# Input projection work placed between the units of linear attention, with gate values and six query tiles kept in DRAM meanwhile

## The chip, the cores and the metric

The kernel runs on one core of a Trainium2 chip. The metric is device microseconds (us) of one execution. The core has five engines that run their own instruction streams in order and meet at semaphores: TensorE (PE, with its weight loads as PEld), VectorE (DVE), ScalarE (ACT), GpSimd (POOL) and SyncE (SP, here only a queue that issues DMAs).

## The reference, cut to what matters

One inference step of a one-layer backbone: a modulated norm, one input projection, two head groups that read it, an output projection and a mixture of experts. Tokens are 128 of context and 1024 latent ones. The part around the change:

```
h = modulate(rms_norm(xc, norm_attn_g[l]), sh1, sc1)
q_g, k_g, v_g, g_g, lora, q_s, k_s, v_s = split_cols(h @ w_in[l])
gla_out, s_f, s_b = gla_branch(q_g, k_g, v_g, g_g, lora, s_zero, s_zero, *gla_p)
...
def gla_branch(...):
    la_f = log_gate(lora_f, wa_f, ba_f)
    la_b = log_gate(lora_b, wa_b, ba_b)
    o_f, s_f = gla_chunked(q, k, v, la_f, s0_f)
    o_b, s_b = gla_chunked(flip(q), flip(k), flip(v), flip(la_b), s0_b)
    o = rms_norm(o_f + flip(o_b), norm_g)
    gate = jax.nn.silu(g.reshape(b, t, GLA_HEADS, GLA_DV).astype(jnp.float32))
    out = (o * gate).reshape(b, t, GLA_WIDTH).astype(g.dtype)
```

The columns of `w_in` have the widths 256, 256, 512, 512, 32, 512, 128, 128 for q, k, v and gate of the gated linear attention (GLA), its low-rank gate input, and q, k, v of the windowed attention. GLA needs q, k, v and the low-rank input; its gate is used only at its very end. The windowed attention's q, k, v are not used in GLA at all. Everything is float32.

## The kernel before

All 1152 tokens are nine tiles (NT) of 128. The program is a row of stages; each closes with a barrier of all engines, so nothing of a stage starts before the last work of the stage ahead. Three stages touch the change.

`project` makes four pieces of modulation (`ada`), normalises and transposes the tokens into `hT`, and runs the projection in the order of its list `items`: q and k (`qk`, three groups of three tiles by four column blocks), `lora`, then `vg`, `gg` and `qs` (nine tiles each, 512 columns) and `kv` (nine tiles, 256 columns). For each tile TensorE runs eight matmuls over the model dimension into one of three banks `psP`, and ScalarE or VectorE moves the bank to its place in SBUF (`by_act`: all `gg`, with Silu, and every second of the others by ScalarE). Weights go through a ring of three buffers `wring` that the SP queue fills.

`linear_attention` works in twelve units `UNITS`: three groups `g` of three tiles by four `m` (direction and pair of heads). For unit `u`:

- TensorE `pre(u)`: gate matmul into the single bank `ps_pre`
- ScalarE `soft(u)`: four activations to `lg`, `ng`; VectorE `cumulate(u)`: running sums and differences into `cum`, `fac`; ScalarE `factors(u)`: exponentials in `fac`
- GpSimd: products `pr`, `kz` and `qi`; VectorE `decayed_keys(u)`: `ksT`
- TensorE `scores(u)` into `ps_a`, `turn_keys(u)` into `ps_kt`; VectorE `keep_scores(u)` copies to `AT`; ScalarE `move_keys(u)` copies `ps_kt` to `ks`
- TensorE `delta(u)` into `ps_d`, kept by VectorE as `S`; after the fourth unit of a group TensorE's `intra(g)` forms `AT` times values

`lg`, `ng`, `pr`, `ksT`, `ks` and `ps_a` have two buffers, so products of a unit can run beside the scores of the one ahead. After the units VectorE runs the recurrence over the tiles (`recur`) and TensorE adds the share of the states tile by tile in `ORDER`. GpSimd closes with `gg` times the norm weights (L654). The order of the work is that in which each engine's code is written.

`window_attention` (L790) turns queries and keys, and per tile does scores, softmax, outputs. Between tiles `ada` (L990) makes eight more pieces of modulation from a ring of three 2 MB buffers `ada_ring`; the same SP queue writes 20 MB of zeros to `sum_rows`. The queue order there is:

```
sp.dma_start(ring[i % RING][:], dram["w_ada"]...[:, :, c0:c0 + 512]).then_inc(ring_in[i % RING], 16)
...
for k in range(*((2 * i, 2 * i + 2) if i < 2 else (i + 2, i + 3))):
```

Of the kernel before, what the change touches and what calls it, by code (L numbers as in the profile page):

```python
# [5 lines left out]
F32 = mybir.dt.float32  # L6
BF16 = mybir.dt.bfloat16
I32 = mybir.dt.int32
ALU = mybir.AluOpType
# [22 lines left out]

def cond_of(t):

    return 0 if t == 0 else 1


def project(nc, dram, keep):

    with ExitStack() as ctx:  # L40
# [6 lines left out]
        RING = 3  # L47
# [3 lines left out]
        row = [sb(f"ada_row{i}", [P, 512]) for i in range(2)]  # L51
        ring = [sb(f"wring{i}", [P, KD, 512]) for i in range(RING)]
        NX = 3
        xin = sb("xin", [P, NX, D])
        xn = sb("xn", [P, 2, D])
        junk = sb("junk", [P, D])
# [3 lines left out]
        hT = sb("hT", [P, KD, T])  # L60
# [8 lines left out]
        ring_in = [sem(f"ring_in{i}") for i in range(RING)]  # L69
# [6 lines left out]
        out_done = sem("kv_out_done")  # L76
# [6 lines left out]
        items = [("ada", i) for i in range(4)]  # L83
        items += [("qk", C_QK), ("lora", C_LORA), ("vg", C_VG), ("gg", C_GG), ("qs", C_QS), ("kv", C_KV)]

        def landed(eng, n):
            eng.wait_ge(ring_in[n % RING], 16 * (n // RING + 1))


        outs = []  # L90
        for kind, what in items:
            if kind in ("qk", "lora"):
                for g in range(3):
                    for m in range(4 if kind == "qk" else 1):
                        outs.append((kind, m, g))
            elif kind != "ada":
                for t in range(NT):
                    outs.append((kind, 0, t))

        def used(eng, n):  # L100

            if items[n][0] == "ada":
                eng.wait_ge(ada_done, items[n][1] + 1)
            else:
                eng.wait_ge(proj_done, max(k for k, o in enumerate(outs) if o[0] == items[n][0]) + 1)

        def dest(kind, m, t):
            if kind == "qk":
                return keep["qkT"][:, m, t * 384:(t + 1) * 384]
            if kind == "lora":  # L110
                return keep["loraT"][:, t * 384:(t + 1) * 384]
            if kind == "qs":

                return keep["qs"][:, t, :].rearrange("p (r g d) -> p g r d", r=4, g=2)
            return keep[kind][:, t, :]

        def source(kind, k):
            if kind == "lora":
                return psP[:, k % NB, 0:384]
            if kind == "qs":  # L120
                return psP[:, k % NB, :].rearrange("p (g r d) -> p g r d", r=4, g=2)
            return psP[:, k % NB, 0:{"qk": 384, "kv": 256}.get(kind, 512)]
# [10 lines left out]
        def _(sp):  # L133
            for n, (kind, what) in enumerate(items):
                if n == 0:
                    sp.dma_start(vec[:], dram["vectors"]).then_inc(vec_in, 16)
                    sp.dma_start(keep["ident"][:], dram["ident"]).then_inc(ident_in, 16)
                if n >= RING:
                    used(sp, n - RING)
                c0, cn = (what * 512, 512) if kind == "ada" else what  # L140
                src = w_ada if kind == "ada" else w_in
                sp.dma_start(ring[n % RING][:, :, 0:cn], src[:, :, c0:c0 + cn]).then_inc(ring_in[n % RING], 16)
# [4 lines left out]
                if n == 4:  # L147
# [5 lines left out]
                    sp.wait_ge(wab_zero, 1)  # L153
                    for strip in range(4):
                        sp.dma_start(keep["wab"][32 * strip:32 * strip + 16, 0:256], dram["gla_wa_f"]).then_inc(later_in, 16)
                        sp.dma_start(keep["wab"][32 * strip + 16:32 * strip + 32, 256:512], dram["gla_wa_b"]).then_inc(later_in, 16)
                    sp.dma_start(keep["gla_mask"][:], dram["gla_mask"]).then_inc(later_in, 16)
                    sp.dma_start(keep["normg"][:], dram["gla_norm_g"].to_broadcast([P, P])).then_inc(later_in, 16)
                    sp.dma_start(keep["S0"][:, 0:2, :], dram["state_f"].rearrange("(m p) v -> p m v", p=P)).then_inc(later_in, 16)
                    sp.dma_start(keep["S0"][:, 2:4, :], dram["state_b"].rearrange("(m p) v -> p m v", p=P)).then_inc(later_in, 16)  # L160

            kv0 = outs.index(("kv", 0, 0))
            sp.wait_ge(evac_act if by_act(kv0) else evac_dve, evacs_before(kv0 + 1, by_act(kv0)))
            sp.dma_start(dram["new_k"], keep["kv"][:, 0, 0:128]).then_inc(out_done, 16)
            sp.dma_start(dram["new_v"], keep["kv"][:, 0, 128:256]).then_inc(out_done, 16)
            sp.wait_ge(out_done, 32)
            sp.wait_ge(later_in, 192)

        @block.tensor
        def _(pe):  # L170
# [4 lines left out]
            def ada(n, i):  # L175

                landed(pe, n)
                if i >= 2:
                    pe.wait_ge(row_kept, i - 1)
                for j in range(KD):  # L180
                    strip = slice(32 * (j % 4), 32 * (j % 4) + 32)
                    last = pe.matmul(psT[strip, i % 2, 0:512], condT[:, j, :], ring[n % RING][:, j, :],
# [23 lines left out]
            for n, (kind, what) in enumerate(items):  # L206
# [9 lines left out]
                landed(pe, n)  # L216
                w = ring[n % RING]
                for kk in range(k, len(outs)):
                    if outs[kk][0] != kind:
                        break  # L220
# [11 lines left out]
                    for j in range(KD):  # L232
                        bank = psP[:, kk % NB, 0:512] if kind == "qs" else source(kind, kk)
# [6 lines left out]
                        else:  # L240
                            last = pe.matmul(bank, hT[:, j, t * P:(t + 1) * P],  # L241
                                             w[:, j, 0:what[1]], start=(j == 0), stop=(j == KD - 1))
# [104 lines left out]
def linear_attention(nc, dram, keep):  # L347
# [9 lines left out]
    with ExitStack() as ctx:  # L357
# [12 lines left out]
        UNITS = [(g, m) for g in range(NG) for m in range(4)]  # L370
# [4 lines left out]
        wab, mask, normg, S0 = keep["wab"], keep["gla_mask"], keep["normg"], keep["S0"]  # L375
        restart = sb("restart", [P, W])
        lg = [sb(f"lg{i}", [P, W]) for i in range(2)]
        ng = [sb(f"ng{i}", [P, W]) for i in range(2)]
# [8 lines left out]
        pr = [sb(f"pr{i}", [P, 4, W]) for i in range(2)]  # L387

        kz = [sb(f"kz{i}", [P, 3, W]) for i in range(4)]
        ksT = [sb(f"ksT{i}", [P, W]) for i in range(2)]  # L390
        ks = [sb(f"ks{i}", [P, G, P]) for i in range(2)]
# [3 lines left out]
        AT = [sb(f"AT{m}", [P, G, 2, P]) for m in range(4)]  # L395
        S = sb("S", [P, 4, NT, P])
        ps_pre = ps("ps_pre", [P, 512])

        ps_a = [ps(f"ps_a{i}", [P, 2, 512]) for i in range(2)]
        ps_t = ps("ps_kt", [P, 512])  # L400
        ps_d = ps("ps_d", [P, 512])
        ps_o = ps("ps_o", [P, 512])

        ps_i = [ps_a[i][:, :, 0:2 * DV].rearrange("p h (m v) -> p h m v", v=DV) for i in range(2)]
# [5 lines left out]
        zeroed, next_in = sem("gla_zeroed"), sem("att_const_in")  # L410
# [23 lines left out]
        def _(sp):  # L434
            sp.dma_start(keep["sink"][:], dram["sink"].to_broadcast([P, 8])).then_inc(next_in, 16)
# [12 lines left out]
        def _(pe):  # L448
# [8 lines left out]
            def scores(u):  # L457
# [4 lines left out]
                if u >= 2:  # L462
                    pe.wait_ge(at_done, u - 1)
# [1852 lines left out]
```

## Time and profile before

| | us |
|---|---|
| median of 3 runs | 1713.17 (1712.33 to 1713.4) |
| the profiled execution | 1710.73 |
| its span | 1708.9 |
| TensorE busy in the span | 1533.5 (90%) |
| VectorE, ScalarE, GpSimd busy | 750.8, 522.4, 591.6 |
| projection, from the start | 334.7 |
| linear attention | 168.9 |
| window attention | 162.2 |

The span runs from the first to the last instruction on the engines. The stages' borders are the starts of the first instruction behind each barrier. In a row of the timeline the first number is the start in us, the second the time to the end of the last of the instructions merged in it, and the bracket the idle time of the engine just before, with what ended it. A float32 matmul shows as two records. A row of a stretch gives busy us and the number of records for each engine, then TensorE's granted clock as a share of 2.4 GHz, the busy share of the DMA engines and GB/s.

### The profile page before, as it was taken

What the parts mean: (1) busy time and instruction counts of PE and PEld (TensorE: products, weight loads), DVE (VectorE), ACT (ScalarE), POOL (GpSimd) and SP (SyncE); (2) the same over time, 40 slices, a digit from 0 to 9 for tenths busy, and PEclk for the clock granted to TensorE, in tenths of its full rate; (3) what the DMA queues carried; (4) which work ended last, traced back from release to release, by engine and by line L of the source; (5) the groups of instructions that cost most, each with busy time, mean ns of one, the idle gap of its engine ahead of it and who ended that gap; (6) DMA issues with size and microseconds to landing.
All of it is one profiled execution on the core that took longest, in us unless ns stands there. A gap on an engine that the chain in (4) does not pass through costs nothing. (4 is left out here: it accounts for less than half of the span.)

```text
span 1708.9 us, 28670 instructions
## 1 busy us (share of the span) xinstructions
PE 1533.5 (90%) x9111; PEld 910.9 (53%) x9112; DVE 750.8 (44%) x1478; ACT 522.4 (31%) x1226; POOL 591.6 (35%) x617
## 2 busy tenths in 40 slices
PE   5999999868769999999999869999999999999734
PEld 2554444646656878455555435555555555555311
DVE  2300000187645656278783324444344444444339
ACT  2400000176506663111110023343343334333312
POOL 0000000076655321111124435555455555555422
PEclk8999999957778999999999979999999999999878
DMA  8320000000019903201200079999999999996477
GB/s 322 104 99 0 25 0 0 30 1 8 1 63 411 380 35 154 92 25 50 86 1 0 0 283 333 338 335 331 343 342 329 336 328 307 263 246 125 70 277 301
DMA packets 93495, 289.50 MB, mean 169 GB/s; under 512 B 12190, under 2 KB 15602, under 8 KB 93170
## 3 DMA queue, kind: packets, MB, share of 16 engines
q1 hardware_dynamic: 66210, 199.96, 30.6%
q0 software_dynamic: 25920, 83.91, 20.4%
q10 hardware_dynamic: 1296, 4.72, 0.7%
q8 instruction: 42, 0.69, 0.2%
q14 instruction: 27, 0.22, 0.0%
HBM read 222.09 MB, written 76.94 MB: 175 GB/s over the span
## 5 line engine op out<-in xcount | busy, mean ns | idle before, releaser
L1952 PE MATMUL ps_g<-w_exp,mix 128*64 x1408 | 326.5, 385 | 5.9 <-DVE own_gu L2047 2.8
L1955 PE MATMUL ps_g<-own_gu,mix 128*64 128x256 f32 x1408 | 326.5, 385 | 0.0
L1952 PEld LDWEIGHTS ps_g<-w_exp,mix 128*64 128x64 f32 x1408 | 187.3, 138 | 107.8 <-issue 11.0
L241 PE MATMUL psP<-wring,hT 128*128 128x512 f32 (+1 forms) x576 | 216.7, 539 | 0.0
L1901 POOL DMA_INDIRECT sum_rows<-mix,scatter_row x66 | 143.5, 2175 | 171.9 <-DVE mix L1990 145.4
L1955 PEld LDWEIGHTS ps_g<-own_gu,mix 128*64 128x64 f32 x1408 | 187.3, 138 | 0.0
L1924 PE MATMUL ps_y<-w_exp,hidT 128*64 x352 | 171.4, 610 | 6.4 <-ACT own_d L2003 6.4
L1925 PE MATMUL ps_y<-own_d,hidT 128*64 128x512 f32 x352 | 171.4, 610 | 0.0
L241 PEld LDWEIGHTS psP<-wring,hT 128*128 128x128 f32 x576 | 109.4, 190 | 107.6 <-issue 103.9
L2047 DVE COPY own_gu<-w_exp 128x2048 f32 x89 | 109.5, 1230 | 62.2 <-issue 39.7
L1874 POOL DMA_INDIRECT mix<-h_rows,gather_row x92 | 98.5, 1071 | 79.0 <-POOL gather_row L1871 40.3
L1326 PE MATMUL ps_o<-wo,mixT 128*128 128x512 f32 x288 | 125.2, 592 | 0.5 <-DVE h L1579 0.5
L628 POOL MEMSET kz<- 128x1152 f32 x4 | 4.0, 1054 | 334.8 <-POOLq L2194 334.8
L1916 PE MATMUL ps_x<-ident,mix 128*128 128x128 f32 x712 | 103.8, 289 | 13.8 <-DMA mix<-h_rows,gather_row 13.8
L1916 PEld LDWEIGHTS ps_x<-ident,mix 128*128 128x128 f32 x712 | 86.7, 194 | 48.5 <-issue 33.8
L2003 ACT ACTIVATE own_d<-w_exp 128x1024 f32 x88 | 93.2, 1059 | 51.5 <-issue 48.6
L2059 DVE SCALAR_TENSOR_TENSOR hid<-silu,tab,ps_g 128x128 f32<-128x128 f32 x88 | 30.6, 347 | 159.7 <-ACT silu L2024 159.7
L1326 PEld LDWEIGHTS ps_o<-wo,mixT 128*128 128x128 f32 x288 | 54.0, 190 | 65.3 <-issue 65.3
L1990 DVE COPY mix<-ps_y 128x512 f32<-128x512 f32 x66 | 45.6, 691 | 80.2 <-PE ps_y L1925 80.2
L1982 DVE COPY mix<-ps_x 128x512 f32<-128x512 f32 x89 | 61.6, 692 | 39.0 <-PE ps_x L1916 39.0
L2003 ACT ACTIVATE mix<-ps_x 128x512 f32<-128x512 f32 x89 | 53.1, 597 | 80.3 <-PE ps_x L1916 80.3
L1924 PEld LDWEIGHTS ps_y<-w_exp,hidT 128*64 128x64 f32 x352 | 41.2, 137 | 68.1 <-issue 57.6
(320 smaller groups left out, 2533.1 us busy)
## 6 DMA issues: line engine op xcount, KB each, us to landing
w_exp<-in_exp_w_gate SPq DMA_DIRECT2D x64, 512.0 KB, 7.6
w_exp<-in_exp_w_up SPq DMA_DIRECT2D x64, 512.0 KB, 12.7
w_exp<-in_exp_w_down SPq DMA_DIRECT2D x64, 512.0 KB, 21.5
sum_rows<-zero_row SPq DMA_DIRECT2D x10, 2048.0 KB, 20.7
sums<-sum_rows SPq DMA_DIRECT2D x36, 512.0 KB, 16.3
ada_ring<-in_w_ada SPq DMA_DIRECT2D x8, 2048.0 KB, 18.7
wring<-in_w_ada SPq DMA_DIRECT2D x4, 2048.0 KB, 14.6
wring<-in_w_in SPq DMA_DIRECT2D x4, 2048.0 KB, 10.7
```

Source lines behind the costliest of these rows:

```text
L241: last = pe.matmul(bank, hT[:, j, t * P:(t + 1) * P], w[:, j, 0:what[1]], start=(j == 0), stop=(j == KD - 1))
L1326: last = pe.matmul(ps_o[:, n, :], mixT[t % 2][:, j, :], wo[:, j, n * 512:(n + 1) * 512], start=(j == 0), stop=(j == KD - 1))
L1874: pool.indirect_dma_start(out=x[k], out_offset=None, in_=dram["h2"], in_offset=bass.IndirectOffsetOnAxis(ap=gi[k][:], axis=0), bounds_chec ...
L1901: pool.indirect_dma_start(out=dram["y"][k % 2], out_offset=bass.IndirectOffsetOnAxis(ap=si[k][:], axis=0), in_=y[k], in_offset=None, bound ...
L1916: last = pe.transpose(ps_x[:, j * P:(j + 1) * P], x[k][:, j:D:KD], keep["ident"][:])
L1924: pe.matmul(ps_y[0:HALF, cols], hT[par][:, 0:HALF], w[:, slot * 3 + 2, cols], start=True, stop=True)
L1925: last = pe.matmul(ps_y[HALF:P, cols], hT[par][:, HALF:P], own_d[:, cols], start=True, stop=True)
L1952: pe.matmul(ps_g[par][0:HALF, 0:2 * FF].rearrange("p (k f) -> p k f", k=2), xT[par][:, j * P:j * P + HALF], w[:, bass.ds(slot * 3, 2), ff] ...
L1955: last = pe.matmul(ps_g[par][HALF:P, 0:2 * FF].rearrange("p (k f) -> p k f", k=2), xT[par][:, j * P + HALF:(j + 1) * P], own_gu[par][:, :, ...
L1982: copy(xT[par][:, half * 512:(half + 1) * 512], ps_x[:, half * 512:(half + 1) * 512]).then_inc(done, 1)
L2003: return act.activation(out, in_, ACT.Copy)
L2047: dve.tensor_copy(own_gu[par][:], w[:, bass.ds((e % NW) * 3, 2), :]).then_inc(own_gu_done, 1)
```

## The change

- `project` keeps `qk`, `lora`, then `gg`, and of `vg` only the three tiles of group 0, as six half tiles of 256 columns (VG_EARLY). Its scratch moves into SBUF that later holds other things; the fourth modulation piece has a buffer of its own (`late`), `lora` too.
- GpSimd multiplies each `gg` tile with the norm weights in `project`, and SP stores the tile to the DRAM tensor `gg_rows`. `window_attention` loads the nine tiles again. Their SBUF holds the states `S` in between.
- The rest are 39 portions (`FILL`) of 256 columns that TensorE runs in `linear_attention`: `vg` half tiles of groups 1 and 2 (12), `qs` half tiles (18), `kv` (9). Six stand between the first gate matmuls, two or three in each of the units 0 to 10 (PER_UNIT, 30), three behind the last values. ScalarE copies each out of one of two half banks `ps_f`. SP loads the weights of the portions during the stage into two halves of `late`.
- `qs` tiles 3 to 8 have no place in SBUF then: ScalarE copies them to three staging buffers, SP stores them to `qs_rows`, `window_attention` loads them.
- To make room, `lg`, `ng`, `pr`, `ksT`, `ks`, `ps_a` become single and `kz` goes from four to two; units run in the order m = 0, 2, 1, 3; `pre` runs three units ahead, not four; `factors(u + 2)` stands ahead of `move_keys(u)`, and `delta(u)` in unit u's own turn.
- In `window_attention` the queue also loads `band` and `cache_v`, which came in the stage before.

```diff
-        items += [("qk", C_QK), ("lora", C_LORA), ("vg", C_VG), ("gg", C_GG), ("qs", C_QS), ("kv", C_KV)]
...
+        ITEMS = [("ada", 0), ("ada", 1), ("ada", 2), ("ada", 3), ("qk", 0), ("lora", 0), ("gg", 0), ("vg", 0), ("vg", 1)]
...
+            for t in range(NT):
+
+                sp.wait_ge(gg_scaled, t + 1)
+                sp.dma_start(dram["gg_rows"][t * P:(t + 1) * P, :], keep["gg"][:, t, :]).then_inc(gg_out, 16)
+            sp.wait_ge(later_in, 16 * 14)
+            sp.wait_ge(gg_out, 16 * NT)
...
+        FILL = [("vg", half, t) for g in (1, 2) for half in range(2) for t in range(g * G, g * G + G)]
+        FILL += [("qs", half, t) for half in range(2) for t in range(NT)] + [("kv", 0, t) for t in range(NT)]
...
+        PER_UNIT = (3, 3, 2, 3, 3, 3, 2, 3, 3, 3, 2)
+        START_FILL = 6
...
+                    if k >= 2:
+                        pe.wait_ge(fill_kept, k - 1)
+                    for j in range(KD):
+                        last = pe.matmul(fill_bank(k), hT[:, j, t * P:(t + 1) * P], keep["late_half"](half)[:, j, :],
+                                         start=(j == 0), stop=(j == KD - 1))
+                    last.then_inc(fill_done, 1)
...
-                if u >= 2:
-                    pool.wait_ge(score_done, u - 1)
+                if u >= 1:
+                    pool.wait_ge(score_done, u)
...
+                at = START_FILL + sum(PER_UNIT[:u])
+                keep_fill(at)
+                if u + 2 < NU:
+                    factors(u + 2)
+                move_keys(u)
+                if u < NU - 1:
+                    keep_fill(at + 1)
                 if u + 3 < NU:
                     soft(u + 3)
-                if u + 2 < NU:
-                    factors(u + 2)
+                if u < NU - 1:
+                    keep_fill(at + PER_UNIT[u] - 1)
+            keep_fill(NF)
```

**TensorE at the start of linear attention.** Before; `ps_pre` is the gate bank, `ps_a` the scores, `ps_kt` the turned keys:

```order
L454 MATMUL ps_pre<-loraT,wab 128x384 x4
L471 MATMUL ps_a<-pr,kz 128x4x16 x2
...
L486 MATMUL ps_a<-pr 64x64 x6
L495 MATMUL ps_kt<-ident,ksT 128x128 x3
L454 MATMUL ps_pre<-loraT,wab 128x384
```

Now; `ps_f` is the portions' bank (16 matmuls are two portions), `ps_td` holds turned keys and the state update:

```order
L512 MATMUL ps_pre<-loraT,wab 128x384
L502 MATMUL ps_f<-late,hT 128x256 x16
...
L528 MATMUL ps_a<-pr,kz 128x4x16 x2
...
L543 MATMUL ps_a<-pr 64x64 x6
L512 MATMUL ps_pre<-loraT,wab 128x384
L551 MATMUL ps_td<-ident,ksT 128x128 x3
L502 MATMUL ps_f<-late,hT 128x256 x8
L565 MATMUL ps_td<-vg,ks 64x128 x6
L502 MATMUL ps_f<-late,hT 128x256 x16
```

One portion now stands between the key turn and the state update that needs the moved keys, and two behind it, ahead of the next scores.

**ScalarE, one unit in the middle of the stage.** Before; `ks` is the key move, `lg` and `ng` the gate activations, `fac` and `elast` the factors:

```order
L604 ACTIVATE elast<-gla_off 128x3
L610 ACTIVATE ks<-ps_kt 128x384
L575 ACTIVATE lg<-ps_pre,vcol 128x384
...
L578 ACTIVATE lg<-lg 128x384
L588 ACTIVATE fac<-fac 128x384
```

Now:

```order
L677 ACTIVATE elast<-gla_off 128x3
L683 ACTIVATE ks<-ps_td 128x384
L705 ACTIVATE vg<-ps_f 128x256
L648 ACTIVATE lg<-ps_pre,vcol 128x384
...
L651 ACTIVATE lg<-lg 128x384
L705 ACTIVATE vg<-ps_f 128x256 x2
L661 ACTIVATE fac<-fac 128x384
```

Three copies of portions stand in a unit's row of activations, one ahead of the gate activations and two ahead of the next factors.

**SP at the start of window attention.** Before:

```order
L875 DMA ada_ring<-in_w_ada 128x8x512
L880 DMA sum_rows<-zero_row 128x4x1024 x2
```

Now:

```order
L977 DMA band<-in_band 128x896
L978 DMA cache_v<-in_cache_v 128x128
L975 DMA mix<-qs_rows 128x512 x2
L984 DMA mix<-gg_rows 128x512 x3
L975 DMA mix<-qs_rows 128x512 x2
L990 DMA ada_ring<-in_w_ada 128x8x512
L995 DMA sum_rows<-zero_row 128x4x1024 x2
L984 DMA mix<-gg_rows 128x512 x3
L975 DMA mix<-qs_rows 128x512 x2
L990 DMA ada_ring<-in_w_ada 128x8x512
```

Loads of 256 KB a tile stand ahead of each of the first pieces of the ring.

## Rows read from the trace of the kernel before

**Rows 1.** Stretches: projection, linear attention, window attention; busy us, records, clock, DMA.

```profile
0.00:334.70 334.70, 311.07 (x985) 164.03 (x986) 36.40 (x87) 45.14 (x99) 0.20 (x4) 0.98 0.20 71
334.70:503.60 168.90, 121.87 (x1340) 99.36 (x1341) 117.57 (x226) 88.28 (x266) 105.04 (x134) 0.70 0.03 9
503.60:665.80 162.20, 153.27 (x1254) 119.09 (x1254) 92.17 (x298) 96.81 (x307) 62.94 (x75) 0.95 0.61 234
```

**Rows 2.** Groups of instructions by form; then the stretch of the last key/value tiles.

```profile
L241 PE MATMUL psP<-wring,hT 128*128 128x256 f32 x144 | 31.2, 379 | 0.0
...
L654 POOL TENSOR_TENSOR mix<-mix,normg 128x512 f32<-128x512 f32 x9 | 11.1, 1277 | 0.0
...
306.40:334.60 28.20, 27.54 (x128) 23.91 (x126) 1.70 (x4) 1.87 (x5) 0.00 (x0) 1.00 0.02 5
```

**Rows 3.** Timeline of TensorE, one unit at full clock; then that stretch.

```profile
410.72 0.44 PE L471 MATMUL ps_a<-pr,kz 64*128 64x64 f32 x4
...
413.69 0.55 PE L495 MATMUL ps_kt<-ident,ksT 128*128 128x128 f32 x3
...
415.63 0.44 PE L471 MATMUL ps_a<-pr,kz 64*128 64x64 f32 x4
...
410.60:418.70 8.10, 8.07 (x163) 6.81 (x161) 7.73 (x19) 1.76 (x6) 2.05 (x3) 1.00 0.01 2
```

**Rows 4.** Waits of TensorE in linear attention; first and last scores in the timeline.

```profile
PE ps_a L471 <- POOL kz L647: 13.2, 7, 3.5
...
356.66 0.69 PE L471 MATMUL ps_a<-pr,kz 64*128 64x64 f32 x4 [3.51 <-POOL kz L647]
...
471.65 0.69 PE L471 MATMUL ps_a<-pr,kz 64*128 64x64 f32 x4 [3.02 <-POOL kz L647]
```

**Rows 5.** Timelines of ScalarE, GpSimd and VectorE in linear attention.

```profile
333.98 0.38 ACT L284 ACTIVATE kv<-psP 128x256 f32<-128x256 f32 x1 [6.52 <-PE psP L241]
...
363.98 0.53 ACT L588 ACTIVATE fac<-fac 128x384 f32<-128x384 f32 x1 [4.72 <-DVE fac L708]
...
368.79 0.47 ACT L610 ACTIVATE ks<-ps_kt 128x384 f32<-128x384 f32 x1
369.16 0.57 ACT L575 ACTIVATE lg<-ps_pre,vcol 128x384 f32<-128x384 f32 x1
...
357.52 3.83 POOL L641 TENSOR_TENSOR pr<-qkT,fac 128x192 f32<-128x192 f32 x4
...
365.23 1.00 POOL L650 TENSOR_TENSOR qi<-qkT,fac 128x384 f32<-128x384 f32 x1
...
341.74 0.56 DVE L682 SCALAR_TENSOR_TENSOR ng<-ng,lg 128x384 f32<-128x384 f32 x1 [2.29 <-ACT lg L578]
...
345.07 0.36 DVE L708 TENSOR_SCALAR fac<-fac 128x384 f32<-128x384 f32 x1
...
356.71 1.67 DVE L694 TENSOR_TENSOR_SCAN lg<-restart,ng 128x384 f32<-128x384 f32 x1 [3.71 <-POOL kz L647]
...
363.24 0.71 DVE L708 TENSOR_SCALAR fac<-fac 128x384 f32<-128x384 f32 x1
```

**Rows 6.** Stretches: three value products, the first state output, and what follows.

```profile
480.80:488.20 7.40, 5.89 (x48) 5.51 (x48) 7.36 (x19) 0.00 (x0) 2.95 (x3) 1.00 0.00 0
488.20:493.20 5.00, 2.06 (x32) 1.86 (x32) 5.00 (x16) 0.00 (x0) 0.00 (x0) 0.92 0.00 0
493.20:499.10 5.90, 5.83 (x54) 5.87 (x56) 2.21 (x4) 0.00 (x0) 0.00 (x0) 0.50 0.01 3
```

**Rows 7.** Timeline of TensorE, the ring's first uses; the stretch up to the second.

```profile
518.35 3.64 PE L990 MATMUL ps_k<-ada_ring,condZ 128*32 128x512 f32 x16
...
532.71 1.92 PE L990 MATMUL ps_k<-ada_ring,condZ 128*32 128x512 f32 x16
...
549.48 1.92 PE L990 MATMUL ps_k<-ada_ring,condZ 128*32 128x512 f32 x16
...
503.60:532.70 29.10, 21.90 (x137) 14.70 (x137) 12.67 (x55) 16.50 (x61) 22.66 (x31) 0.71 0.99 377
```

More of the change, by code:

```diff
@@ L50, in project @@
         modA1 = sb("modA1", [P, KD, 2])
[L51 to L52 removed]
+        row = [keep["gg"][:, NT - 2 + i, :] for i in range(2)]
+        slots = [sb(f"wring{i}", [P, KD, 512]) for i in range(3)]
+        slots.append(keep["late"][:].rearrange("p (j n) -> p j n", n=512))
+        wlora = sb("wlora", [P, KD, 32])
+        normg = sb("normg", [P, P])
         NX = 3
[L54 removed]
+        xin = keep["mix"][:, NT * 512:NT * 512 + NX * D].rearrange("p (i n) -> p i n", n=D)
+        junk = keep["mix"][:, NT * 512 + NX * D:NT * 512 + (NX + 1) * D]
         xn = sb("xn", [P, 2, D])
[L56 removed]
         ssq = sb("ssq", [P, NT])
@@ L81, in project @@
         w_in = dram["w_in"].rearrange("(j p) n -> p j n", p=P)
-        items = [("ada", i) for i in range(4)]
-        items += [("qk", C_QK), ("lora", C_LORA), ("vg", C_VG), ("gg", C_GG), ("qs", C_QS), ("kv", C_KV)]
[L86 to L105, printed above, removed]
+        ITEMS = [("ada", 0), ("ada", 1), ("ada", 2), ("ada", 3), ("qk", 0), ("lora", 0), ("gg", 0), ("vg", 0), ("vg", 1)]
+        item_in = [sem(f"w_in_{kind}{i}") for kind, i in ITEMS]
+        weights = [slots[0][:], slots[1][:], slots[2][:], slots[3], slots[0][:], wlora[:], slots[1][:],
+                   keep["late_half"](0), keep["late_half"](1)]
+        columns = [None, None, None, None, C_QK, C_LORA, C_GG, (C_VG[0], 256), (C_VG[0] + 256, 256)]
+        outs = [("qk", m, g) for g in range(3) for m in range(4)] + [("lora", 0, g) for g in range(3)]
+        outs += [("gg", 0, t) for t in range(NT)] + [("vg", half, t) for half in range(2) for t in range(VG_EARLY)]
         def dest(kind, m, t):
@@ L133, in _ @@
         def _(sp):
[L134 to L140, printed above, removed]
+            sp.dma_start(vec[:], dram["vectors"]).then_inc(vec_in, 16)
+            sp.dma_start(keep["ident"][:], dram["ident"]).then_inc(ident_in, 16)
+            for n, (kind, what) in enumerate(ITEMS):
+                if n in (4, 6):
+                    sp.wait_ge(ada_done, n // 2 - 1)
+                if n == 7:
+                    sp.wait_ge(ada_done, 4)
+                c0, cn = (what * 512, 512) if kind == "ada" else columns[n]
                 src = w_ada if kind == "ada" else w_in
-                sp.dma_start(ring[n % RING][:, :, 0:cn], src[:, :, c0:c0 + cn]).then_inc(ring_in[n % RING], 16)
+                sp.dma_start(weights[n], src[:, :, c0:c0 + cn]).then_inc(item_in[n], 16)
                 if n == 1:
@@ L181, in ada @@
                     strip = slice(32 * (j % 4), 32 * (j % 4) + 32)
-                    last = pe.matmul(psT[strip, i % 2, 0:512], condT[:, j, :], ring[n % RING][:, j, :],
+                    last = pe.matmul(psT[strip, i % 2, 0:512], condT[:, j, :], weights[n][:, j, :],
                                      start=(j < 4), stop=(j >= 4))
@@ L205, in _ @@
             k = 0
-            for n, (kind, what) in enumerate(items):
+            for n, (kind, what) in enumerate(ITEMS):
                 if kind == "ada":
@@ L215, in _ @@
                     continue
-                landed(pe, n)
-                w = ring[n % RING]
+                pe.wait_ge(item_in[n], 16)
+                w = weights[n]
                 for kk in range(k, len(outs)):
-                    if outs[kk][0] != kind:
+                    if outs[kk][0] != kind or (kind == "vg" and outs[kk][1] != what):
                         break
```

359 lines of the change are left out of this document (229 added, 130 removed).

## Prediction, made before the changed kernel was run

> **What bounds the kernel now.** I first cut the span into stages with the table of stretches [rows 1]. The input projection keeps TensorE busy for 311.1 of its 334.7 us at a granted clock of 0.98: it is bound by TensorE alone. Linear attention takes 168.9 us, but TensorE is busy for only 121.9 of them, at a mean granted clock of 0.70, so part of even this busy time is matmuls at the lower of the two levels. Window attention is TensorE's again: 153.3 of 162.2 us. So the projection needs an engine that linear attention leaves idle. The engines run in order and the stages are separated by a barrier, so the idle time can only be used by work written into the stage, which is what the change does.
>
> Next I read how big the movable pieces are [rows 2]. The last eight key/value tiles, 256 columns wide, fill 306.40 to 334.60, busy 27.54 us at clock 1.00: 3.45 us each (nine tiles are 144 records of 379 ns that overlap). A tile of 512 columns has matmuls twice as long, so 6.9 us.
>
> Then a unit of linear attention at the full clock [rows 3]. A unit (three token tiles by one of four pairs of heads and direction) is scores 410.72 to 413.69, then key turn, the gate's matmul and the state update up to the next scores at 415.63: 4.91 us. Twelve make 58.9 us, though from the first scores to the last, 356.66 to 471.65 [rows 4], the stage needs 10.5 us a unit. What ends the waits is the feeding chain [rows 4]: TensorE waits most for GpSimd's products (13.2 us in 7 waits), and the first scores start only at 356.66.
>
> **What is moved, and what it is worth in the projection.** 12 half tiles of the gla values, 18 half tiles of the window queries and 9 key/value tiles leave: 39 portions of 256 columns. 39 x 3.45 = **134.6 us less** in a stage that TensorE bounds. The gate values now come before the rest, and GpSimd scales them there: nine operations of about 1.3 us [rows 2] against a tile every 6.9 us, and nine stores behind them, the last with six half tiles (20.7 us) left as cover. Without that cover a store's landing would lie in front of the barrier, 2 to 4 us. At the start the same weights are asked for in nearly the same order; the fourth modulation piece no longer waits for a buffer, and the narrow low-rank weights stand ahead of six loads of x. I take 0, and -1 to +2 for the range.
>
> **What TensorE does in linear attention now.** Its work at the full clock: units 58.9; nine value products, 5.89 us for three in the row of 480.80, so 17.7; eight outputs from the states, 2.06 us each in the row of 488.20, 16.5 less some overlap, I take 16 [rows 6]; portions 134.6. Sum **227.2 us**. This is more than the 168.9 us of the stage, so if the clock is high TensorE is now the bound, and the rest of the stage's length is what it still waits.
>
> *Opening.* Before, 22 us of the stage pass until the first scores at 356.66 [rows 4]. Now six portions (20.7 us) and three gate matmuls stand there, so they cover it. ScalarE reads a portion before the second gate's activations, and these wait for the single gate buffer: about 3 us later than before. Idle 1 to 2 us.
>
> *A full unit.* Between scores and scores stand 4.91 + 3 x 3.45 = 15.3 us. Products (GpSimd, 7.7 us from 357.52 to 365.2, the store of the query factor 1 us behind) now have one buffer and start only after the scores before: 3.0 + 7.7 = 10.7 us after a unit's start, or 12 with the last product. That is under 15.3: the second buffer's loss is hidden by the portions. Take the portions away and these 11 to 12 us would be the unit's length, against 10.5 now.
>
> *The loop through ScalarE and VectorE* [rows 5]. ScalarE does the factors of unit u+2 (363.98 to 368.79, 4.8 us), then moves the keys of unit u (0.4), then the gate activations of u+3 (369.16, four activations, 2.2 us), and now three copies of portions at 0.38 us. VectorE's running sums stand between activation and factors: 341.74 to 345.4 is 3.7 us with GpSimd idle, 356.71 to 363.95 is 7.2 us with GpSimd busy, and 0.6 belongs to the second before its first row. In the new order GpSimd works from 3 to 12 us after a unit's start and the sums mostly after that; I take 4.8, nearer the free row. Loop: 4.8 + 0.4 + 2.2 + 1.2 + 4.8 = 13.4 us, and some tenths for signals, under 15.3. Where a unit has only two portions (three of eleven), 11.9 us of TensorE's work meet a loop of about 14: there the state update waits for the keys 1 to 3 us, and so does the one behind it. Written out for eleven units this is 11 to 13 us of waits.
>
> *End.* The last value product waits for VectorE as now (1.5 to 2 us). The three portions left (10.3 us) stand over most of the chain through the states, for which TensorE was idle for 2.9 of the 5.0 us before 493.20 [rows 6]. Barrier, first gate matmul and last sum as before: 3 us.
>
> *Clock.* With 1.5 us of idle time in 480.80 to 488.20 it stayed at 1.00; a wait of 3 us before 493.20 was followed by 5.9 us at 0.50 [rows 6]. One or two waits of the new stage may reach that length: 2 us.
>
> Stage: 227.2 + 1.4 + 12.5 + 1.8 + 3 + 2 = 247.9, which I round down to **246 us**, as the pieces of TensorE overlap by some tenths at each seam (the first 384-column matmul of a unit starts inside the transposes). Against 168.9: **+77 us**. Weights for the moved portions are loaded in this stage in pieces of 512 B a partition and reuse a half buffer; the first is free after the third portion of unit 0 and wanted at unit 2, more than 15 us for 1 MB. The twelve 128 KB stores of staged queries have three buffers, 10 us each. I charge nothing; the queue is almost idle there (share 0.03 [rows 1]).
>
> **Window attention: a queue that was full gets 4.5 MB more.** Its ring of modulation weights (2.1 MB each) is used at 518.35, 532.71 and 549.48 [rows 7], and the queue delivers 377 GB/s up to the second use. The second piece lies behind four transfers, 8.39 MB. Now 12.06 MB must have landed: band and cached values 0.53, six query tiles 1.57, six gate tiles 1.57 more. By 532.71 it is 11.0 MB. 1.1 MB at 377 to 410 GB/s is a **wait of 3 us on TensorE**, which no slack takes up; the third piece has 4.46 MB in front of it, and 10.9 us at 410 GB/s meet a slack of about 7.6, nearly the same 3. With a little lower clock behind the wait: **+4 us**, 0 to 9. The Trainium skill, DMA: Bandwidth & Descriptors, section Bandwidth, asks for transfers of at least 1 MiB for 75% of the peak, and these are of 256 KB; no row here shows such loads in a full queue. By that rule the 4.46 MB would take a third longer, 3 to 4 us more, and the sum would be 3 to 4 us higher.
>
> **Sum.** -134.6 + 77 + 4 = -53.6 against the profiled execution's own 1710.7 us, whose span is 1708.9: 1657.1. The three timed runs have their median 2.4 us above that execution, so 1659.5, **forecast 1660 us**.
>
> **Rivals.** *The feeding loop is the bound.* If VectorE's sums meet GpSimd's products, the loop is 13.4 + 2.4 = 15.8 us and in the short units further from 11.9: 0.5 us in eight units, 4 in three, and the waits behind them: 8 to 15 us more, **1671 us**. Before the change they met in nearly every unit, which speaks for it; the new gaps of GpSimd speak against. The Trainium skill, SBUF — State Buffer, section Who interferes with whom, states that a VectorE instruction with two SBUF inputs contends with a GpSimd instruction that reads SBUF; the 7.2 us against 3.7 agree with that, and it sides with this rival only as far as the two do meet.
>
> *No overlap.* If each portion lies where its unit's chain is waiting for TensorE itself (keys turned, then a portion before the state update), idle time stays and the work merely moves: 0, plus 4 in window attention, **1717 us**. The in-order queue makes this possible; the 15.3 us over 10.7 and 13.4 speak against it.
>
> *The clock stays low: slower.* The stage ran at 0.70. If the many small matmuls keep it there although TensorE has no idle time, 227.2 / 0.70 = 325 us and 3 at the edges: 328 - 168.9 - 134.6 + 4 = +28, **1741 us**. It decides below a mean clock of 0.8: then 227.2 / 0.8 + 15 = 299 eats the 134.6 + 168.9 - 4. Against it: 410.60 to 418.70, small matmuls without an idle moment, had 1.00 [rows 3].
>
> **How the numbers follow.** Forecast, 1640 to 1668: 0.68. Feeding loop, 1665 to 1685: 0.19. No overlap: 0.05, half of it within 0.2% of 1713. Low clock: 0.08. The low end is the sum with no waits and no charge in window attention (227.2 + 4 = 231: 1640); the high end is the feeding loop with 9 us in window attention and 5 for the clock: 1685, which I take to 1690. Range **1640 to 1690**. Faster by over 0.2% (about what a measurement can tell from no change): 0.88; same 0.03; slower 0.09.
>
> **What the profile after would show.** Projection ending near 200 us; linear attention 240 to 250 us long with TensorE over 90% busy and a clock over 0.95; unit to unit 15 to 16 us, state updates waiting 1 to 4 us for ScalarE's keys after the short units, scores never for GpSimd; in window attention one wait of 2 to 5 us for the second ring piece. Waits for keys in every unit mean the loop; a clock under 0.8 the slow case; a late end of the projection would mean that I misread the start or the stores.

## The result, and the profile after

The changed kernel takes 1658.7 us (median of 4 runs, 1655.5 to 1661.7) against 1712.75 us; the ratio is 0.968 with a 95% interval of 0.967 to 0.970. A second set of five runs gave 1657.0 us and 0.969 (0.967 to 0.971). The prediction was 1660 us. The profiled execution has 1656.29 us and a span of 1654.5 us, 54.4 less than before.

The three stages of the kernel after, as stretches (us, busy us and records of TensorE, weight loads, VectorE, ScalarE, GpSimd, then clock, DMA share, GB/s), which answer to [rows 1]:

```profile
0.00:200.40 200.40, 177.02 (x649) 101.34 (x650) 29.07 (x76) 39.66 (x89) 11.65 (x13) 0.96 0.33 116
200.40:440.80 240.40, 227.07 (x1964) 193.91 (x1964) 102.26 (x226) 101.96 (x304) 83.68 (x122) 0.97 0.08 23
440.80:609.70 168.90, 153.34 (x1254) 118.71 (x1254) 91.10 (x298) 96.80 (x307) 63.01 (x75) 0.94 0.65 251
```

The projection is 134.3 us shorter. Linear attention is 71.5 us longer and TensorE is busy for 94% of it, at a clock of 0.97 instead of 0.70. Window attention is 6.7 us longer, the rest of the program 1.7, which no experiment below takes apart. Together -134.3 + 71.5 + 6.7 + 1.7 = -54.4.

TensorE's waits in linear attention (waiting instruction, releaser: us in total, times, longest), against [rows 4]:

```profile
PE ps_td L565 <- ACT ks L683: 9.9, 4, 3.7
...
PE ps_a L528 <- POOL kz L753: 0.8, 1, 0.8
```

GpSimd's products, the first wait before with 13.2 us, hold TensorE up once, at the opening. What is left are state updates that wait for moved keys. Where they stand, in TensorE's timeline (start, us to the end of the last merged one, idle before):

```profile
263.61 3.62 PE L502 MATMUL ps_f<-late,hT 128*128 128x256 f32 x16
267.16 0.88 PE L565 MATMUL ps_td<-vg,ks 128*64 128x128 f32 x12
267.97 3.72 PE L502 MATMUL ps_f<-late,hT 128*128 128x256 f32 x16
...
304.01 1.55 PE L565 MATMUL ps_td<-vg,ks 128*64 128x128 f32 x12 [3.67 <-ACT ks L683]
...
373.40 1.55 PE L565 MATMUL ps_td<-vg,ks 128*64 128x128 f32 x12 [3.67 <-ACT ks L683]
```

The rows at 263 to 268 are the normal case: portion, state update, portion, with no idle time, 3.55 us from a portion to the next instruction. The two long waits stand in the first unit of the second and of the third group. What happens ahead of the first of them, on VectorE, ScalarE and GpSimd:

```profile
287.54 0.69 DVE L840 COPY vg<-ps_o 128x512 f32<-128x512 f32 x1 [4.55 <-PE ps_o L577]
292.78 0.69 DVE L840 COPY vg<-ps_o 128x512 f32<-128x512 f32 x1 [4.55 <-PE ps_o L577]
293.39 0.55 DVE L784 SCALAR_TENSOR_TENSOR ng<-ng,lg 128x384 f32<-128x384 f32 x1
...
297.93 0.71 DVE L810 TENSOR_SCALAR fac<-fac 128x384 f32<-128x384 f32 x1
...
298.67 0.53 ACT L661 ACTIVATE fac<-fac 128x384 f32<-128x384 f32 x1 [7.29 <-DVE fac L810]
...
303.48 0.47 ACT L683 ACTIVATE ks<-ps_td 128x384 f32<-128x384 f32 x1
...
295.87 2.55 POOL L747 TENSOR_TENSOR pr<-qkT,fac 128x192 f32<-128x192 f32 x4 [14.37 <-PE ps_a L543]
```

VectorE stands idle twice for 4.55 us at a copy of values that TensorE has yet to form, since a portion lies between each two value products. Only then do its sums start; ScalarE has waited 7.29 us for them, runs 4.8 us of factors and moves the keys last. That TensorE lacks them is the end of a chain that began at its own value products.

Behind these two waits the clock is low:

```profile
303.90:310.00 6.10, 5.99 (x29) 5.05 (x30) 4.15 (x9) 2.31 (x6) 0.00 (x0) 0.73 0.06 21
373.30:379.50 6.20, 6.10 (x24) 4.92 (x25) 4.26 (x10) 2.30 (x6) 0.00 (x0) 0.55 0.06 21
```

In window attention, SP's issues, TensorE's second use of the ring, and the stretch of 29.3 us from the stage's start, against [rows 7]:

```profile
441.67 0.90 SPq L975 DMA_DIRECT2D mix<-qs_rows  x2
442.61 1.38 SPq L984 DMA_DIRECT2D mix<-gg_rows  x3
...
457.53 1.49 SPq L990 DMA_DIRECT2D ada_ring<-in_w_ada  x1
...
475.02 3.33 PE L1110 MATMUL ps_k<-ada_ring,condZ 128*32 128x512 f32 x16 [5.99 <-DMA ada_ring<-in_w_ada]
...
440.80:470.10 29.30, 20.58 (x137) 14.13 (x137) 13.77 (x59) 16.34 (x61) 23.84 (x31) 0.77 0.99 371
```

TensorE waits 6.0 us for the second ring piece and does the piece at the lower clock for most of its length (3.33 us for 1.92). The third use comes 18.2 us behind it and the fourth 18.6 us behind the third; they wait for nothing.

### The profile page after: what moved, and what is told of

Its sections match the earlier page's. It is cut to its first block and busy times, and to the rows that moved or that the text cites. A ratio compares the mean times of both kernels' runs of the same rounds, so it can differ in the third digit from the quotient of the medians.

```text
span 1654.5 us, 29332 instructions
## 1 busy us (share of the span) xinstructions
PE 1506.5 (91%) x9399; PEld 943.3 (57%) x9400; DVE 727.7 (44%) x1467; ACT 530.6 (32%) x1255; POOL 566.1 (34%) x615
## 5 line engine op out<-in xcount | busy, mean ns | idle before, releaser
L2025 POOL DMA_INDIRECT sum_rows<-mix,scatter_row x66 | 127.7, 1935 | 173.0 <-DVE mix L2114 146.4
L502 PE MATMUL ps_f<-late,hT 128*128 128x256 f32 x624 | 144.7, 389 | 0.0
L502 PEld LDWEIGHTS ps_f<-late,hT 128*128 128x128 f32 x624 | 119.8, 195 | 18.6 <-issue 1.9
L1641 POOL TENSOR_TENSOR h<-h,rows 128x1024 f32<-128x1024 f32 x9 | 21.1, 2349 | 156.3 <-DVE h L1710 156.3
## 6 DMA issues: line engine op xcount, KB each, us to landing
wring<-in_w_ada SPq DMA_DIRECT2D x3, 2048.0 KB, 13.1
```

The source lines that it names most:

```text
L502: last = pe.matmul(fill_bank(k), hT[:, j, t * P:(t + 1) * P], keep["late_half"](half)[:, j, :], start=(j == 0), stop=(j == KD - 1))
L2025: pool.indirect_dma_start(out=dram["y"][k % 2], out_offset=bass.IndirectOffsetOnAxis(ap=si[k][:], axis=0), in_=y[k], in_offset=None, bound ...
```

## The experiments

Where lengths of stages are compared, linear attention is measured from GpSimd's first memset in it to that in window attention, and window attention from there to the first load behind it. The lengths are those of one profiled execution each. The kernel before was timed again beside each group of kernels: 1711.5 us (beside changed again, ring first, sums first and 1/8), 1710.1 (ring and sums, keys first, gates last, 1/2) and 1711.7 (ring and keys, all three). The ratios are to these. The portions of 1/8 ran twice, those of 1/2 once.

| kernel | median us of 5 runs | ratio to before (95%) | linear attention | window attention |
|---|---|---|---|---|
| before | | | 168.3 | 162.3 |
| changed, again | 1657.0 | 0.969 (0.967 to 0.971) | 239.7 | 170.9 |
| ring first | 1649.7 | 0.964 (0.963 to 0.966) | 239.8 | 161.5 |
| sums first | 1643.8 | 0.960 (0.959 to 0.962) | 226.3 | 169.5 |
| ring and sums | 1639.2 | 0.958 (0.956 to 0.960) | 228.0 | 162.5 |
| keys first | 1642.2 | 0.960 (0.958 to 0.962) | 224.0 | 170.1 |
| gates last | 1664.9 | 0.973 (0.972 to 0.975) | 242.2 | 170.5 |
| ring and keys | 1636.6 | 0.956 (0.955 to 0.958) | 224.0 | 162.8 |
| all three | 1633.2 | 0.954 (0.953 to 0.956) | 224.0 | 162.9 |
| portions of 1/8 | | | 200.4 | |
| portions of 1/2 | | | 204.5 | |

**The yardstick.**

> The changed kernel as it is, as the yardstick of this call. Its four timed runs lay at 1655.5 to 1661.7 us, two near 1656 and two near 1661. Both theories expect 1656 to 1662 us again; if the profiled execution is one of the longer ones, its stages show where the 5 us lie.

Its runs lay between 1656.3 and 1664.2 us, so the medians of the other kernels are read against 1657 to 1659 us. The waits for keys are the same 9.9 us in four; the ring's wait is 5.5 us. Its profiled execution (1660.1 us) was 4 us longer than the first one (1656.3), and 2 of these lie in window attention (170.9 against 168.9).

**Ring first.** The zeros are issued behind the third ring piece:

```diff
...
-                if i == 0:
-                    sp.wait_ge(zeroed, 1)
-                for k in range(*((2 * i, 2 * i + 2) if i < 2 else (i + 2, i + 3))):
+                if i == RING - 1:
+                    sp.wait_ge(zeroed, 1)
+                    for k in range(RING):
+                        zeros(k)
+                if i >= RING:
+                    zeros(i)
```

> Only the order of the queue in window attention is changed: the three first ring pieces are issued ahead of the 10 MB of zeros that stood between them. Theory (the queue is full and the second piece is late by the bytes in front of it): the wait of 6.0 us for the second ring piece goes, window attention shrinks from 168.9 to about 162 us, the time falls by 6 to 8 us. Rival (the small loads of gates and queries slow down window attention by other waits, as GpSimd's for gates): the wait goes and the time falls by less than 3 us.

1649.7 us, 7.3 less. The wait is gone from the list, and the stage has its old length with all the new loads in it:

```profile
441.20:602.70 161.50, 151.91 (x1254) 118.54 (x1254) 91.03 (x298) 96.62 (x307) 62.98 (x75) 0.96 0.68 263
```

With the queue in the old order the stage took 168.9 to 170.9 us in every profiled execution, so it gains 7 to 9. The loads of gates and queries cost nothing by themselves; they cost what they put in front of a piece that TensorE needs. Zeros that are wanted only at the stage's end stood there too: 4.2 MB ahead of the second piece and 8.4 MB ahead of the third (not 10 MB, as I had written).

**Sums first.**

```diff
-                if u + 2 < NU:
+                if u + 2 < NU and not (u and UNITS[u - 1][1] == 3):
                     cumulate(u + 2)
...
-                    for t in range(g * G, g * G + G):
-                        keep_intra_of(t)
+                    keep_intra_of(g * G)
+                    cumulate(u + 3)
+                    keep_intra_of(g * G + 1)
+                    keep_intra_of(g * G + 2)
```

> Only VectorE's order at the end of a group is changed: the running sums of unit u+3 come ahead of the second and third copy of the values. Theory (the two waits of 3.67 us for moved keys come from VectorE standing at value copies that wait for TensorE, so that sums and factors start late): both waits go, with the lower clock behind them, 8 to 12 us less in all. Rival (ScalarE's new work, the copies of portions and the factors ahead of the key move, makes them): the waits stay within 0.5 us and the time is unchanged.

1643.8 us, 13.1 less, a little over the expected 8 to 12. The stretch, TensorE's waits and VectorE's timeline:

```profile
201.00:427.96 226.96, 221.08 (x1964) 189.65 (x1964) 99.65 (x226) 102.07 (x304) 82.85 (x122) 1.00 0.08 24
...
PE ps_td L565 <- ACT ks L683: 2.5, 2, 2.0
...
281.14 0.69 DVE L840 COPY vg<-ps_o 128x512 f32<-128x512 f32 x1 [1.42 <-PE ps_o L577]
281.75 0.55 DVE L784 SCALAR_TENSOR_TENSOR ng<-ng,lg 128x384 f32<-128x384 f32 x1
...
285.07 0.36 DVE L810 TENSOR_SCALAR fac<-fac 128x384 f32<-128x384 f32 x1
...
286.38 0.69 DVE L840 COPY vg<-ps_o 128x512 f32<-128x512 f32 x1 [0.95 <-PE ps_o L577]
```

The sums fill VectorE's idle time between two copies. Both long waits went: 7.3 us. The records of TensorE are the same 1964, but their busy time fell from 227.07 to 221.08 us and the clock is 1.00: another 6.0 us that were not waiting but work at the lower clock. Not all of it belongs to the two waits, though; the run of both edits, below, parts it.

**Keys first**, VectorE's order left as in the change:

```diff
+                move_keys(u)
                 if u + 2 < NU:
                     factors(u + 2)
-                move_keys(u)
```

> One part of the change undone: ScalarE moves the keys of unit u ahead of the factors of u+2, VectorE's order stays as in the changed kernel. Theory A (the waits of 9.9 us arise because the key move stands behind factors that wait for late sums): the state update never waits more than 0.7 us, linear attention shrinks by 12 to 14 us as with the sums first. Theory B (late sums are a limit of their own, since products need the factors): the wait only moves to the scores, and the gain is under 5 us.

1642.2 us, 14.8 less; theory A. ScalarE's and TensorE's timelines at the same place, and the stretch:

```profile
292.59 0.49 ACT L683 ACTIVATE ks<-ps_td 128x384 f32<-128x384 f32 x1 [5.54 <-PE ps_td L551]
294.34 0.52 ACT L661 ACTIVATE fac<-fac 128x384 f32<-128x384 f32 x1 [1.26 <-DVE fac L810]
...
295.94 0.88 PE L565 MATMUL ps_td<-vg,ks 128*64 128x128 f32 x12
...
200.10:424.60 224.50, 220.87 (x1964) 189.65 (x1964) 103.25 (x226) 101.75 (x304) 84.29 (x122) 1.00 0.08 24
```

ScalarE moves the keys while it would wait for the late sums, and the state update at 295.94 finds them. So late sums alone do no harm. The two long waits need both, late sums and a key move behind the factors, and either edit cures them. The stage is 15.7 us shorter, more than the 12 to 14 expected, and 2.3 shorter than with the sums first. The reason is the wait of 1.96 us in the first unit, which stays with the sums first and goes here. There the sums are not the cause: ScalarE does the factors of two units back to back and moves the keys last. From the changed kernel:

```profile
224.31 0.51 ACT L661 ACTIVATE fac<-fac 128x384 f32<-128x384 f32 x1
...
229.12 0.52 ACT L661 ACTIVATE fac<-fac 128x384 f32<-128x384 f32 x1
...
233.93 0.47 ACT L683 ACTIVATE ks<-ps_td 128x384 f32<-128x384 f32 x1
```

So a key move behind the factors does cost by itself, once, where two rounds of factors meet. TensorE is now busy for 220.9 of 224.5 us.

**Gates last.** The early half tiles of values are projected ahead of the gates, and their weights are loaded ahead of those of the gates:

```diff
...
-        outs += [("gg", 0, t) for t in range(NT)] + [("vg", half, t) for half in range(2) for t in range(VG_EARLY)]
+        outs += [("vg", half, t) for half in range(2) for t in range(VG_EARLY)] + [("gg", 0, t) for t in range(NT)]
```

> The gate values are projected behind the six early half tiles of values, so the last gate tile's product and store have no cover ahead of the barrier. Theory (the prediction's price for the missing cover): the projection ends 2 to 4 us later, the time rises by 2 to 4 us. Rival (the barrier waits for the stores anyway or not at all): unchanged within 1 us.

1664.9 us, 6 to 8 more, where 2 to 4 were expected. TensorE's first instruction behind the barrier:

```profile
206.51 1.62 PE L512 MATMUL ps_pre<-loraT,wab 128*128 128x384 f32 x2 [5.18 <-PEq L2320]
```

It comes after 5.18 us without work, against 1.46 in the changed kernel: 3.7 us, within the stated price. But it then takes 1.62 us for 0.88, the lower clock, and linear attention is 2.5 us longer, all of it TensorE's busy time (229.6 us for 227.1). The expected price was that of the barrier alone. In the profiled execution the stage also starts later by 1.7 us that the edit did not make: they lie in one row of the query and key projection, 7.47 us at 46.88 for 5.82 at 46.84 in the changed kernel, ahead of everything that was moved.

**Portions of 1/8 and of 1/2.** The loop over the model dimension runs once, or four times, of eight:

```diff
-                    for j in range(KD):
+                    for j in range(1):
...
```

> Each portion runs one of its eight matmuls, so 7/8 of the 134.6 us of moved work, 117.7 us, is left out; everything else, copies and stores too, stays. If TensorE's own work sets the stage, it shrinks by the whole 117.7 us, from 240.4 to 123 us. Theory: without the portions the single buffers show, products after scores (3.0 + 8.7 us) or the loop over ScalarE and VectorE (13.4 us) set a unit of 12 to 14 us, so the stage is 175 to 195 us, longer than the 168.9 us of the kernel before, and the time falls by only 45 to 65 us. Rival (lost buffers cost nothing even bare): about 165 us.

> Each portion runs four of its eight matmuls: 67.3 us of moved work is left out, 67.3 us stays. With one of eight the stage took 201 us, with all 240.4. Theory (under the portions lies a chain of its own, of about 200 us): TensorE's work of 154 us fits in, so the stage stays at 200 to 208 us, and the first half of the portions is nearly free. Rival (each portion costs its length wherever it stands): halfway by length, 17 + 50 us of portions, 218 us. Its experts get other tokens, so only the stage is to be read, not the whole time.

```profile
199.00:399.97 200.97, 140.25 (x1418) 110.80 (x1418) 104.79 (x226) 101.02 (x304) 85.33 (x122) 0.75 0.09 27
...
PE ps_td L565 <- ACT ks L683: 36.1, 10, 7.8
PE ps_a L528 <- POOL kz L753: 9.2, 4, 4.7
```

```profile
200.80:405.90 205.10, 169.69 (x1652) 140.54 (x1652) 105.23 (x226) 101.51 (x304) 84.57 (x122) 0.92 0.09 26
...
PE ps_td L565 <- ACT ks L683: 23.8, 9, 5.5
```

The first fence is that of 1/8, the second that of 1/2. With seven eighths of the portions' matmuls gone the stage falls by 39 us, not by 118, to 200.4 us; I had expected 175 to 195. It is 32 us longer than before the change, with 17 us of portions (at the full clock) in it: with little to hide them, the single buffers and the new order cost 15 us or more, and waits for keys in ten of twelve units show where. Which buffer or which order makes them was not run. The second to fourth eighth, 50 us of work at the full clock, make the stage 4 us longer. The last four, 67 us, make it 35 us longer. Sums first and keys first take 13 and 16 us off the full stage; what they would do at 1/2 was not run. In both kernels the experts work on other tokens than in the real one: with 1/8 the part behind window attention takes 1068 us against 1045, so my expectation for the whole time (45 to 65 us less) was badly put: it came out at 17 less, which was a miss, and the whole time says nothing of the portions.

**Together.**

> Both edits together, the ring pieces ahead of the zeros and VectorE's sums ahead of the second and third copy. They act in different stages, so both theories of cause expect the sum: 7 us and 13 us less than the changed kernel, 1636 to 1639 us. If the ring's wait depended on when linear attention ends, the sum would fall short.

> Ring pieces ahead of the zeros and the keys moved ahead of the factors, VectorE's order as in the changed kernel. The gains of the two stages add (7 and 15 us): 1634 to 1637 us, linear attention 224 to 226 us.

> All three edits. Theory (late sums cost only through the key move that stood behind them, and the key move no longer does): the sums first bring nothing on top, within 1 us of the run with ring and keys alone. Rival (they bring products earlier too): 2 to 4 us less.

1639.2 us for ring and sums, 17.8 less where the parts give 20. Its window attention is 1.0 us longer than with the ring first alone, and its linear attention 1.7 us longer than with the sums alone. For the latter one place shows why, in the profiled executions: the 32 records behind the first, shorter wait for keys, which neither edit touches. First ring and sums, with the stage's stretch, then sums first:

```profile
233.81 0.88 PE L565 MATMUL ps_td<-vg,ks 128*64 128x128 f32 x12 [1.96 <-ACT ks L683]
234.61 8.86 PE L502 MATMUL ps_f<-late,hT 128*128 128x256 f32 x32
...
199.80:428.40 228.60, 222.76 (x1964) 190.84 (x1964) 99.67 (x226) 102.11 (x304) 82.89 (x122) 0.99 0.08 24
```

```profile
235.00 0.88 PE L565 MATMUL ps_td<-vg,ks 128*64 128x128 f32 x12 [1.96 <-ACT ks L683]
235.81 7.17 PE L502 MATMUL ps_f<-late,hT 128*128 128x256 f32 x32
```

The same wait of 1.96 us was followed by 8.86 us in one execution and 7.17 in the other. The changed kernel shows the 8.86 too, in both of its profiled executions, and so does ring first. So of the 6.0 us of lower clock that sums first did not have, 1.7 are this chance and 4.3 (227.07 - 222.76) belong to the two long waits: 7.3 us idle and 4.3 behind them, 11.6 in all. With the 1.96 us of the first unit and its 1.7 this makes 15.3, near the 15.7 of keys first.

1636.6 us for ring and keys, 20.4 less where they give 22, with linear attention at 224.0 us as expected. With all three the two stages have the same lengths to 0.1 us. Its median is 3.4 us lower, 1633.2, but its profiled execution is 2 us longer in span than that of ring and keys (1634.0 against 1631.9), and the runs overlap (1631.5 to 1635.8, 1633.7 to 1636.9). By the two stages the theory holds: the sums add nothing on top of the keys. By the median alone the result lies outside the theory's 1 us and within the rival's 2 to 4, and where the 3.4 us are from stays open. The best version is 1.4% faster than the changed kernel and 4.6% faster than the one before.

## Why the prediction was right, and where it was not

**The removed term.** 134.6 us for 39 portions, measured 134.3. The projection had no other bound close behind TensorE: its idle time is 23.4 us, for 23.6 before. That scaling and stores would lie under the six half tiles held, and gates last gives the price when they don't.

**TensorE as the new bound.** That TensorE would set the stage held. The sum of its work at the full clock was 227.2 us; at a clock of 1.00 the stage's records take 221.1 (sums first) and 220.9 (keys first), so the sum was 6 us too high. The main reason is a misread row. The 2.06 us at 488.20 hold 32 records, and these are two outputs from the states, not one: the two lines of this product have 128 records for eight outputs, before and after. From the kernel before, then the first and the last row of all eight in the changed kernel:

```profile
L551 PE MATMUL ps_a<-S,qi 64*128 64x128 f32 x64 | 8.6, 346 | 3.0 <-DVE vg L787 3.0
...
L551 PE MATMUL ps_a<-S,qkT 64*128 64x128 f32 x64 | 8.1, 332 | 0.0
```

```profile
430.96 0.49 PE L625 MATMUL ps_a<-mix,qi 64*128 64x128 f32 x4
...
438.72 0.42 PE L625 MATMUL ps_td<-S,qkT 64*128 64x128 f32 x4
```

Eight outputs take 8.2 us, where I had 16. The value products were 1 us too high as well. Against this a portion between other matmuls takes 3.55 us from start to start and not 3.45, which makes the 39 portions 3 us longer. My rounding down by 1.9 us, which I put down to seams, took back a part of it. In the changed kernel the lower clock adds 6.0 us (227.07), where I had charged 2. Outputs counted at twice their time and a clock charged at a third cancel, and that is luck.

**The waits.** Of 18.7 us charged, 13.3 us of idle time were there: 9.9 at the keys against 12.5, 0.8 at the opening against 1.4, nothing at the last value product against 1.8. The remaining 2.6 are the barriers and edges, for which I had 3. So 5.4 us were charged too much, and with the cancelled errors above this is why the stage came out at 240.4 and not 246. The size of the waits was near, the place was wrong. I had put the waits behind the units with two portions, where TensorE comes round before the loop through ScalarE and VectorE. Only 0.6 us came there, in the last unit, behind the last short one. Three quarters (7.3 of 9.9 us) came in the first unit of the second and of the third group, from a step that the prediction never wrote out: VectorE's three value copies in its in-order queue ahead of the next sums, with portions now between the products that they wait for. The other 2.0 us are those of the first unit, where two rounds of factors meet on ScalarE. The check that I named for the case, waits "after the short units", would have failed.

**The feeding loop.** I took 4.8 us for the sums, between 3.7 with GpSimd idle and 7.2 with it busy. These two rows were not of the same kind: half of the units run one operation more (0.6 us), and the 7.2 is one of them. In nine of the twelve units of the changed kernel GpSimd is idle during the sums, and they take 3.7 or 4.3 us. As they met in only three, the rival of 1671 us did not come. The row at 293.39 is one of the three: it needs 5.2 us to 298.6, with GpSimd at work from 295.87, where in sums first the same operations need 3.7 us from 281.75 to 285.4. The Trainium skill, SBUF — State Buffer, section Who interferes with whom, names contention of a VectorE instruction with two SBUF inputs and a GpSimd read. The rows agree for the subtractions, which have two inputs (1.91 us for 1.50), but that is 0.4 of the 1.6 us. The other 1.1 fall on the TENSOR_SCALAR rows behind them, which read one tensor (0.71 us for 0.36 in the row at 297.93), and the sentence on two inputs does not cover these. The subtractions, in the changed kernel and in sums first:

```profile
294.96 1.91 DVE L804 TENSOR_TENSOR fac<-cum 128x384 f32<-128x384 f32 x3
...
283.32 1.50 DVE L804 TENSOR_TENSOR fac<-cum 128x384 f32<-128x384 f32 x3
```

**No overlap, and the low clock.** The net gain of 54 us rules the first out, and the thin portions show the overlap itself: 50 us of work, the second to fourth eighth, cost 4 us. The second rival fell with the mean clock of 0.97. The Trainium skill, TensorE: Matmul & The Clock Gate, section What's actually happening, says that the slow state is the default and that activity releases it. The trace agrees: the mean clock of the stage was 0.70 with gaps, 0.75 with thin portions, 0.92 with half and 1.00 where the long waits were gone. The first matmuls of a unit's scores (144 records in each kernel) took 350 ns on average before, 361 with thin portions, 284 with half and 280 in the changed kernel. So the thin portions did not speed them up and the thicker ones did. A good part of the gain is this: before, TensorE was busy for 121.9 us with the stage's own work. In keys first all 39 portions take 137 us of the 220.9, which leaves 84 for the same work.

**Window attention.** The mechanism and the piece were right, the term mis-sized: a wait of 6.0 us for 3, +6.7 us for +4. TensorE came to the second piece 28.2 us after the stage's start and not 29.1, with a clock of 0.77 up to there and not 0.71. The queue delivered 371 GB/s, 10.9 MB in 29.3 us; the other 1.2 MB of the 12.06 at 409 GB/s would be through at 32.2 us, yet TensorE goes on at 34.2. So 0.9 us of the 3 missing are the earlier use and 2.0 lie between the byte count and the release, by landing or by transfers issued later that share the queue, which no run separates. By the release the queue had moved 12.8 MB, so it was not idle meanwhile. For the third piece I had nearly the same 3 us; it came in time, as TensorE was late itself. The rule of the Trainium skill, DMA: Bandwidth & Descriptors, section Bandwidth, on transfers of at least 1 MiB, named in the prediction, gives as an estimate a third more time for the 4.5 MB. With it the sum would have met the 6.0 us, but the trace does not agree with its reason: the queue moved 371 GB/s with the small loads, against 377 without.

**The total.** The terms were -134.6, +77 and +4, and the stages gave -134.3, +71.5 and +6.7, with 1.7 more behind them. The forecast of 1660 us for 1658.7 is nearer than its parts: one stage was charged 5.5 us too much, and two places 4.4 too little.

## What to carry to other kernels

Work moved into an idle engine's gaps can be nearly free until the engine's sum nears the chain underneath (here 50 us for 4), and it can even speed up what is there by keeping the clock high. Beyond that point it costs (here 67 us for 35), and the room made for it costs too (here 15 us or more when the stage ran nearly bare), so add up all three before deciding how much to move. Count the records of a row before multiplying it. Once the engine is the bound, follow every in-order queue through the odd iteration (end of a group, first of the next): a copy that waits for a product behind new work delays all that its engine does next. And in a full DMA queue, ask of each transfer when it is needed: zeros for the end of a stage in front of weights for its middle cost as much as the loads one meant to add.

## What the runs showed of the hardware

A wait of 3.7 us cost more than one and a half times its length: two of them were 7.3 us of idle time and 4.3 us more of later work (clock 0.73 and 0.55 in the 6 us behind them). And a wait of 1.96 us, at the same place and of the same length, was followed by the lower clock in four executions (1.7 us more) and not in a fifth. I had charged 2 us for the whole stage, where 6 were due.

VectorE operations that read a single tensor can be slowed while GpSimd works: the TENSOR_SCALAR at 297.93 took 0.71 us in the changed kernel and 0.36 with GpSimd idle in sums first. And fourteen loads of 64 to 448 KB, set between transfers of 2 MB in a full queue, left its rate at 371 GB/s, against 377 without them.
